# One decoder step: projections by quarters of their rows, the last FFN round tile by tile, and 84 adaLN tiles between the products of the input projection

## The reference, cut to what matters

```
mod = silu(c) @ w_ada + b_ada                 # (9 sequences, 12288); w_ada is 2048 x 12288
sh1, sc1, g1, sh2, sc2, g2 = split(mod, 6)    # 2048 each
h = rmsnorm(x, g_pre_mix) * (1 + sc1) + sh1
m = mixer(h)      # proj = h @ w_in (2048 x 5632, and 16 columns dt); conv, SSD scan, stick-breaking
                  # attention over 64 cache pages; concat(y, o) @ w_out (2048 x 2048)
x = x + g1 * rmsnorm(m, g_post_mix)
h = rmsnorm(x, g_pre_ffn) * (1 + sc2) + sh2
f = conv_ffn(h)   # h @ w_ffn_in (2048 x 11264), conv, silu(gate) * val, @ w_ffn_out (5632 x 2048)
x = x + g2 * rmsnorm(f, g_post_ffn)
```

## Time and profile before

| stretch, us from the span's start | what | PE busy, us | PE clock granted |
|---|---|---|---|
| 0 to 113 | 32 adaLN tiles, transposes, first norm | 67.35 | 0.85 |
| 113 to 129 | last fold, first part of h | 3.78 | 0.50 |
| 129 to 478 | input projection, 44 products and 44 adaLN tiles | 347.52 | 0.99 |
| 478 to 952 | attention, SSD scan, one adaLN group | 356.14 | 0.77 |
| 952 to 1075 | output projection, 16 products and 16 adaLN tiles | 123.00 | 0.98 |
| 1075 to 1118 | residual, norm, second h | 20.89 | 0.84 |
| 1118 to 1940 | FFN except its last 4 units | 821.16 | 1.00 |
| 1940 to 2010.4 | last 4 units, residual, output | 48.61 | 0.77 |

### The profile page before, as it was taken

How to read it: one execution, slowest core, us unless ns; L and a number is a source line. 1 busy time by engine, 2 the same in 40 slices (tenths; PEclk the granted TensorE clock), 3 DMA queues, 4 the chain that set the end, 5 groups by cost and what they waited for, 6 DMA issues and landing times.

```text
span 2010.4 us, 31591 instructions
## 1 busy us (share of the span) xinstructions
PE 1788.4 (89%) x13853; PEld 1584.5 (79%) x13853; DVE 942.2 (47%) x1212; ACT 653.1 (32%) x607; POOL 52.8 (3%) x146
## 2 busy tenths in 40 slices
PE   3869999997667887885997799999999999999986
PEld 2348998896545665453996799999999999999985
DVE  0052323323665332535234756566566566566554
ACT  1132222223633342113222543333333333333332
POOL 1000000000000000010000000000000000000001
PEclk9869999998678895587999899999999999999997
DMA  9966887884058993036674344444444454544431
GB/s 325 340 240 225 287 281 261 278 282 161 3 186 304 367 361 102 0 116 230 231 279 160 105 152 165 167 168 168 165 159 162 165 167 168 168 164 160 160 104 63
DMA packets 185180, 389.49 MB, mean 194 GB/s; under 512 B 9692, under 2 KB 18572, under 8 KB 184458
## 3 DMA queue, kind: packets, MB, share of 16 engines
q1 hardware_dynamic: 178816, 373.32, 53.8%
q0 software_dynamic: 2592, 10.42, 1.4%
q10 hardware_dynamic: 3634, 3.74, 0.6%
HBM read 377.03 MB, written 10.41 MB: 193 GB/s over the span
## 4 chain that ended last, share of the span: by engine, by line
PE 80%; DVE 9%; DMA 4%; ACT 4%; issue 2%; ACTq 1%; SPq 0%; POOL 0%; DVEq 0%; POOLq 0%
PE ps L667 20%; PE ps L668 20%; PE ps L669 20%; PE ps L623 4%; PE ps L642 4%; DMA araw<-in_w_ada_dram 2%; PE ps L864 2%; PE ps L735 1%; PE ps L1004 1%; ACTq L1163 1%; PE ps L897 1%; PE ps L631 1%; PE ps L995 1%; PE ps L1052 1%; DVE xraw L1676 1%
## 5 line engine op out<-in xcount | busy, mean ns | idle before, releaser
L1481 DVE TENSOR_TENSOR wlo<-raw,whi 128x2048 fp32r<-128x2048 f32 x192 | 438.2, 2289 | 441.3 <-ACT whi L1208 440.9
L1208 ACT ACTIVATE whi<-raw 128x2048 fp32r<-128x2048 f32 x192 | 367.0, 1915 | 665.1 <-PE ps L669 372.5
L667 PE MATMUL ps<-h2hi,whi 128*128 128x288 f32 x1408 | 416.7, 296 | 12.3 <-DVE wlo L1481 12.3
L668 PE MATMUL ps<-h2lo,whi 128*128 128x288 f32 x1408 | 417.4, 296 | 0.0
L669 PE MATMUL ps<-h2hi,wlo 128*128 128x288 f32 x1408 | 416.6, 296 | 0.0
L667 PEld LDWEIGHTS ps<-h2hi,whi 128*128 128x128 f32 x1408 | 268.2, 190 | 12.9 <-issue 11.9
L669 PEld LDWEIGHTS ps<-h2hi,wlo 128*128 128x128 f32 x1408 | 264.6, 188 | 0.0
L668 PEld LDWEIGHTS ps<-h2lo,whi 128*128 128x128 f32 x1408 | 264.5, 188 | 0.0
L667 PE MATMUL ps<-hhi,whi 128*128 128x288 f32 x704 | 211.5, 300 | 11.7 <-DVE wlo L1481 11.7
L667 PE MATMUL ps<-ghi,whi 128*128 128x288 f32 x704 | 209.0, 297 | 5.5 <-DVE wlo L1481 5.5
L668 PE MATMUL ps<-hlo,whi 128*128 128x288 f32 x704 | 210.5, 299 | 0.0
(11 more groups left out here) (373 smaller groups left out, 2122.1 us busy)
## 6 DMA issues: line engine op xcount, KB each, us to landing
raw<-in_w_ffn_in_dram SPq DMA_DIRECT2D x88, 1024.0 KB, 5.0
raw<-in_w_ada_dram SPq DMA_DIRECT2D x64, 1024.0 KB, 6.6
raw<-in_w_in_dram SPq DMA_DIRECT2D x44, 1024.0 KB, 8.5
raw<-in_w_ffn_out_dram SPq DMA_DIRECT2D x44, 1024.0 KB, 5.0
araw<-in_w_ada_dram SPq DMA_DIRECT2D x32, 1024.0 KB, 13.9
kring<-in_cache_k_dram SPq DMA_DIRECT2D x64, 512.0 KB, 5.8
vring<-in_cache_v_dram SPq DMA_DIRECT2D x64, 512.0 KB, 5.9
raw<-in_w_out_dram SPq DMA_DIRECT2D x16, 1024.0 KB, 5.8
```

What stands on the lines that cost most here:

```text
L667: mm(o, whi[:, high, q, cols], xh, start=(first and q == 0), stop=False)
L668: mm(o, whi[:, high, q, cols], xl, start=False, stop=False)
L1208: fn(whi[:, g % HIGH], raw[:, ring.slot[u]], ACT.Copy).then_inc(hi_ready, 1)
L1481: tt(wlo[:, slot], raw[:, slot], whi[:, g % HIGH].bitcast(F32), SUB).then_inc(lo_ready, 1)
```

## The change

**The ring's kinds.** Only 2 adaLN groups (8 tiles) come first. The input projection's string is `("ggaaaa" * 5 + "ga") * 4`: 44 products and 84 adaLN tiles. The one group before the output projection stays; the output projection is 16 products without adaLN tiles. The sum, 96 adaLN tiles, is the same, and so are the 5 slots. The order of adaLN groups is changed so that the parts of sc1 and sh1 come in quarters.

**Projections by quarters of their rows.** All 11 column groups are multiplied with the first quarter of the rows (4 chunks), then all with the second, and so on. Each product is complete in PSUM and is taken out in two pairs of tiles, over 3 pairs of banks: in the first quarter ACT copies them to `proj` (or mT), in the others DVE adds them. h is made by quarters too, within the adaLN tiles number 16, 24 and 32, and the dt columns are multiplied by quarters. The output projection takes its quarters in the order 2, 3, 0, 1 (attention's rows first).

**Input loads.** x comes ahead of the parameter vectors in ACT's queue; the last 8 small loads move from ACT's queue to GpSimd's. The inputs' state rows are transposed after the first 8 adaLN tiles.

**The end.** The last down units are multiplied tile by tile (16 tiles of 12 matmuls, three PSUM banks), into a second hi/lo buffer (`ghi2`, `glo2`). Beside them PE transposes x (already final) and gainT*f into token rows; the sum of squares is gathered per tile, the root is taken on three short columns, and DVE makes the output with six operations `y = g * r + x`. SP writes it out in six pieces.

The core of the diff:

```
-    FIRST, PROJ, BETWEEN = 8 * RING, 2 * PROJ_GROUPS * RING, RING
-    ring = Ring("a" * FIRST + "ggaa" * (PROJ // 4) + "a" * BETWEEN + "ggaa" * (RING * KC // MC // 2) + "g" * (3 * RING * FC // MC),
+    FIRST, BETWEEN = 2 * RING, RING
+    MIXER = ("ggaaaa" * (PROJ_GROUPS // 2) + "ga") * QUARTERS
+    OUTPUT = "g" * (QUARTERS * OUT_GROUPS)
+    ring = Ring("a" * FIRST + MIXER + "a" * BETWEEN + OUTPUT + "g" * (3 * RING * FC // MC),
                 FIRST, WIDE, DEEP, (FIRST, BEFORE_OUT))
...
# PE
+            def fold():
+                n = pos.folded + 1
+                pe.wait_ge(ada_row, n)
...
+            def ada():
+                group, j = divmod(pos.ada, RING)
+                if j == 0 and group > pos.folded:
+                    fold()
+                if j == 2 and group % 2 == 0 and dts[0] < QUARTERS and group == 2 * (dts[0] + 1):
+                    dt_products()
...
+            for kind in MIXER:
+                if kind == "a":
+                    ada()
+                else:
+                    if pos.g % PROJ_GROUPS == 0:
+                        pe.wait_ge(h_lo, pos.g // PROJ_GROUPS + 1)
+                    product(lambda k: (hhi[:, k, :], hlo[:, k, :]))
...
# ACT, input projection
+                if kind == "a":
+                    if a in (16, 24, 32):
+                        modulate(hf[:], hhi, SH1, a // 8 - 1)
+                    a += 1
+                else:
+                    q, g = product_of(n)
+                    if q == 0:
+                        for i in range(2):
+                            from_psum(proj[:, MC * g + 2 * i:MC * g + 2 * i + 2, :], n, i)
+                    if n + 2 < QUARTERS * PROJ_GROUPS:
+                        hi()
+                    n += 1
...
# DVE, input projection
+            def ada(a):
+                group, j = divmod(a, RING)
+                if j == 0 and group > pos.folded:
+                    mod_of()
+                if a in (16, 24, 32):
+                    quarter(a // 8 - 1)
+                if j == 3:
+                    if dts[0] < QUARTERS and group == 2 * (dts[0] + 1):
+                        dt_part()
+                    rows_of()
...
+                else:
+                    q, g = product_of(n)
+                    if n + 1 < QUARTERS * PROJ_GROUPS:
+                        lo()
+                    if q:
+                        for i in range(2):
+                            from_psum(proj[:, MC * g + 2 * i:MC * g + 2 * i + 2, :], n, i)
+                    n += 1
...
# DVE, output projection: after y's low part (y_lo)
+            rows_of()
+            lo()
+            n, a = QUARTERS * PROJ_GROUPS, FIRST + MIXER.count("a") + BETWEEN
...
# PE, the end
+            for j in range(KC):
+                f_tile(j)
+                if j == 0:
+                    conv_rows()
+                if 1 <= j <= 12:
+                    if j == 1:
+                        pe.wait_ge(fc_o, 2)
+                    x2_rows(j - 1)
+                if j >= 3:
+                    gf_rows(j - 3)
...
# DVE, the end
+            for t in range(NT + 1):
+                w = P if t < NT else TS
+                r = rtok[0:w, t:t + 1]
+                early, late = x2tok[0:w, t, 0:DM - GC], x2tok[0:w, t, DM - GC:DM]
+                stt(early, gtok[0:w, t, :], r, early, MUL, ADD).then_inc(y_ready, 1)
+                stt(late, ps[0:w, 5 + t, :], r, late, MUL, ADD).then_inc(y_ready, 1)
```

More of the change, by code:

```diff
@@ L645, in ada_unit, with product @@
                 pos.u += 1
-            def adaq(bank, fold_last=True):
-                pe.wait_ge(group_free, pos.group + 1)
-                if fold_last:
-                    fold(bank)
-                for j in range(RING):
-                    ada_unit(bank, j)
                 pos.ada += 1
-            def unit3(bank0, xs, first, last, before=lambda m: None):
+            def product(x):
                 u, g = pos.u, pos.g
@@ L661, in unit3 @@
                 for m in range(MC):
-                    before(m)
+                    p = 2 * g + m // 2
+                    if m % 2 == 0 and p >= 3:
+                        pe.wait_ge(*evacuated(p - 3))
+                    o = ps[:, 2 * (p % 3) + m % 2, 0:T]
+                    cols = slice(m * P, (m + 1) * P)
+                    for q in range(QC):
+                        xh, xl = x(product_of(g)[0] * QC + q)
+                        mm(o, whi[:, high, q, cols], xh, start=(q == 0), stop=False)
+                        mm(o, whi[:, high, q, cols], xl, start=False, stop=False)
+                        i = mm(o, wlo[:, slot, q, cols], xh, start=False, stop=(q == QC - 1))
+                    if m == 1:
+                        i.then_inc(pair_full, 1)
+                i.then_inc(w_used, 1)
+                pos.u += 1
+                pos.g += 1
+            def unit3(bank0, xs, first, last):
+                u, g = pos.u, pos.g
+                slot, high = ring.slot[u], g % HIGH
+                pe.wait_ge(lo_ready, g + 1)
+                for m in range(MC):
                     for q in range(QC):
@@ L1138, in _ @@
+            pe.wait_ge(tile_summed, KC)
+            for t in range(NT + 1):
+                w = P if t < NT else TS
+                i = mm(ps[0:w, 3, t:t + 1], fsum[:, t * P:t * P + w], ones[:, 0:1], start=True, stop=True)
+            i.then_inc(sum_ready, 1)
         @block.scalar
@@ new lines, in _ @@
+            for j in range(KC):
+                if j in (1, 3, 5):
+                    lo()
+                if j in (7, 11, 15):
+                    rows_of_gf((j - 7) // 4)
+                tile(j)
+                if j:
+                    total(j - 1)
+            total(KC - 1)
+            norms[0] += 1
+            dve.wait_ge(root_ready, norms[0])
+            dve.reciprocal(rtok[:, 0:NT], rtok[:, 0:NT])
+            c.link(dve.reciprocal(rtok[0:TS, NT:NT + 1], rtok[0:TS, NT:NT + 1]))
```

693 lines of the change are left out of this document (404 added, 289 removed).

## The result

The changed kernel takes 2208.56 us (median of 4 runs, 2208.12 to 2217.18), the kernel before 2014.97 in the same session. The ratio is 1.0964, with a 95% interval of 1.0928 to 1.1: slower by 9.6%. The forecast was 2206, the range 2120 to 2250.

What follows compares the result with a forecast made beforehand. The prediction took the start as bound by loading 32 adaLN tiles and the input projection by PE. Start -61, input +286, output -20 and end -11 sum to +194, giving 2206 us, range 2120 to 2250.

Steps and rivals of the forecast that it cites:

- The input projection: First product to last copy and fold: 635 us against 349 before, +286 us; bounds 550 and 672.
- the late load: Input projection, 20 block ends: the next load waits for the second product's slot; next product at 9.5 us after it.
- DVE's order: Input projection, quarters 2 to 4: fold waits for `rows_of`, which DVE reaches after the next `lo`; some 80 us.
- the clock: Input projection: PE restarts at half clock after each gap, some 2.4 us more each, some 57 us in all.
- E: Input projection: the moment a block's second product ends, before which the next block's first load can't be issued.
- The start: Up to the first input product: 68 us against 129.00, -61 us; bounds 58 and 90.
- The output projection: First product 0.7 us later, held by DVE's order; root at 1066.5 against 1086.41, -20 us.
- The end: Last FFN round to span's end: idle gap gone, smaller last operations and store, -11 us; 0 to 16 gained.
- The late load alone: Rival, input projection: `rows_of` does not hold the fold in quarters 2 to 4; 2125 us, chance 0.13.
- The clock staying up: Rival, input projection: PE's gaps do not lower its clock; 2149 us, chance 0.09.
- The start not won: Rival, start: GpSimd issues its 8 loads late and the state rows arrive late; 2231 us, chance 0.08.
- The loads hidden: Rival, input projection: slots come free earlier or loads are short, so it takes its work, 391 us; 1965 us, chance 0.05.

Runs made afterwards that it cites:

- e2: Changed kernel with DVE making the next block's first low part behind the block's four adaLN steps instead of ahead of them; 2118.94 us.
- e3: Changed kernel with PE's gaps in the input projection filled by matmuls of the identity into a free PSUM bank; 2169.36 us.
- e5: Changed kernel with period 5 ("ggaaa") instead of 6 in the input projection and 20 adaLN tiles moved to the output projection; 2071.06 us.
- e10: Changed kernel with period 4, 44 adaLN tiles in the input projection, 40 in the output projection, and the edit of e9; 2039.38 us.
- e8: Changed kernel with the eight small loads put back from GpSimd's queue to the end of ACT's queue; 2219.87 us.
- e9: Changed kernel with the first output unit's high part, row copy and low part made ahead of y's high and low parts; 2204.16 us.
- e7: Kernel before with only the new last FFN round and end, plus merged semaphores; 1996.08 us, ratio 0.9899.
- e1: Changed kernel with the same 84 adaLN tiles spread evenly, one product then two tiles ("gaa"), in the input projection; 2082.08 us.

## Why the prediction was right

**The input projection.** All three steps (the late load, DVE's order, the clock) are shown. The profile after agrees with the parts of the sum, from the end of a pair to the next product:

| block | predicted | measured |
|---|---|---|
| quarter 1, plain | 9.5 | 9.7, 9.6, 9.4 |
| quarter 1, with a quarter of h | 23.3 with its slow beginning | 21.7, 24.3 |
| quarter 2 | 15.4 | 15.1 to 16.3 |
| quarter 3 | 17.3 | 16.7 to 16.9 |
| quarter 4 | 18.3 | 17.7 to 18.3 |

The fold in quarter 3 came at E + 11.4 (489.34 to 500.75), 11.6 predicted. PE was busy 450.4 us in the window; the work at full clock is 391 by the prediction's count, so some 59 us are the slow clock, 57 predicted. The rest, 187 us, is idle. The stage took 636.6 us; 635 was said. Within the 57 the parts are less exact: behind a plain gap of quarter 1 a pair of products took 1.3 to 1.7 us more than the 13.0 at full clock, not 2.4, and in quarters 2 and 3 it took 1.5 to 1.9 and 0.4 to 0.9 us more, where 0.6 and nothing were put down. And "PE busy about six tenths", among the signs, does not follow from the prediction's own sum: 391 and 57 of 635 are 0.71, as measured (450.4 of 637).

That these are causes and not only sizes that fit, the runs show: without DVE's wait 90 us less (e2; 80 said), with the clock held up 39 to 45 less (e3), and with the ring's slot free in time 192 less in the stage for 20 tiles fewer (e5), 273 less for 40 (e10). The three are not independent: each gap both idles PE and lowers its clock, so e2's 90 us hold a part of the clock's, some 19 us by PE's busy time.

**The Trainium skill's rule on the clock** (TensorE: Matmul & The Clock Gate, What's actually happening) would have taken the slow beginning as under 1% of the span. Here the lower level cost 59 us by the count, 2.7% of the span, because it was paid after each of 20 gaps and not once. The measurement decides against carrying the rule over to a kernel whose gaps come back.

**The start** was mis-sized: 72.9 against 68, -56.1 against -61. I had the fourth tile's load done at 24 us; PE could use it only at 27.61:

```profile
27.61 1.94 PE L706 MATMUL ps<-araw,cs 128*32 128x512 f32 x8 [1.11 <-DMA araw<-in_w_ada_dram]
```

The root came at 48.05, some 4 us late, and the rest of the chain ran as described. The step of the issuing (8 loads on POOL, no wait of 19 us) was right, but worth only 6 us (e8): with c ready early, PE waits for the landing of the second, third and fourth tile (4.63, 3.85 and 1.11 us).

**The output projection**: from 134.5 to 113.7, -20.9 against -20; the first product to the root 113.66, 114 said. That DVE's order would hold the first product back is right, and e9 shows what it cost: 7.0 us.

**The end** was mis-sized: -17.7 against -11, beyond my bound of -16. By the prediction's steps the last of the six operations would end 52.4 us after the last round's beginning (1939.9 to 1992.3); it took 49.9 (2162.57 to 2212.5). PE was busy 39.2 us, as counted (25.7 and 13.5), and idle 2.8, so the handshakes didn't bind; but the last tile's sum, square, transposes and root lay almost wholly beside that work, and the first of the six operations began 42.7 us after the round, not some 45. The larger part is the last store: I kept 7 us from the 8.5 of before, and 2.8 passed from the last operation's end to the span's. Rows of the changed kernel's end:

```profile
2205.28 1.82 DVE L2202 SCALAR_TENSOR_TENSOR x2tok<-gtok,rtok,x2tok 128x1536 f32<-128x1536 f32 x1
...
2211.79 0.73 DVE L2203 SCALAR_TENSOR_TENSOR x2tok<-ps,rtok,x2tok 32x512 f32<-32x512 f32 x1
2211.89 0.98 SPq L509 DMA_DIRECT2D out_dram<-x2tok  x2
```

**Everything else** was put at 0 and came out at +11.5 in the one profiled execution; by the spread between the traces above neither of its two parts can be put down to the change. The other terms were off by +5 (start), +2 (input), -1 (output) and -7 (end), which cancel: between the medians lie 193.6 us, 194 in the forecast. That the total came so close is partly this luck: the two mis-sized terms are 5 and 7 us of 194. The 204.9 us between the two profiled spans are 11 more, most of it because the changed kernel's profiled execution was the slowest of its four.

**The rivals.** The late load alone (2125) is what e2 measured, 2118.94: in the changed kernel it is not so, because of the order of two lines. The clock staying up (2149) is e3, at 2169. The start not won is out (its 2231 was 25 us over the forecast, though the bound of 90 us for the start gives 22). The loads hidden (1965) would need a sixth slot; a kernel with six slots was not tried. e10 comes nearest: hidden loads with a shorter period, at the price of tiles in the output.

**Where the tiles cost least.** Taking 24 adaLN tiles out of the start won at most 50 us (56.1 less the 6 of e8), 2.1 us a tile. A tile in the output projection cost 2.1 (e5) to 2.6 us (e10). With period 4 the input projection's 44 tiles cost little more than their 0.95 each (e10); with period 6 the 20 tiles beyond period 5 cost 9.6 us each (192 / 20). So the change saved at 2.1 a tile and paid up to 9.6. No distribution tried here beat the 32 at the start and 44 + 16 behind, and the part of the change that wins by itself is its end (e7).

## What to carry to other kernels

Count a ring's slots against the period of the pattern that runs through it: a load whose slot is freed by the last unit of a burst can't start before the burst is over, and then its whole way (here 5.1 us of loading, 1.9 and 2.3 for the two parts) lies in the gap. Then read each engine's program in order for what stands behind that late unit; work whose data are long there is late with it, and moving one step gave back 90 of the 288 us that the stage had lost. A gap that comes back every 30 us is paid twice, as idle time and as a lower clock after it, so price the pair.

## What the runs showed of the hardware that was not expected

- An idle time of 2.46 us behind two adaLN tiles was enough for the granted clock to fall to its 1.2 GHz level (e1, windows at 426 and 428 us: 0.60, 0.55). Of two of 2.25 us one lowered it and one did not (0.50 at 386 us, 1.00 at 406).
- A 1 MiB load reached ACT 5.10 us after its issue when alone and 6.94 us after it when another had been issued 1.02 us before it.
- With PE never idle and the clock at 1.00, single executions of equal instructions differ by 0.8% in rate (374 or 377 matmuls in 50 us). It is a property of the execution: both values occur among kernels with the same FFN.
- The last store, 32 rows x 512 columns in SP's queue, has its issue done at 2212.87, 2.4 us before the span ends; before, with 32 x 2048 in GpSimd's queue, it was 8.0 (2002.37 to 2010.4). Which of the two, size or queue, makes the difference was not tried.
